# Where the background work stands between the expert rows of a hybrid decoder step: searches just in time, the mixer's second half in the middle periods

## The reference

```
h   = rmsnorm(x);  proj = h @ w_in                       # 1024 x 9240
o_a = gla(q, k, v, log_a)                                # 4 heads, state 128x256
o_b = mlstm(conv(q), conv(k), v, i, f)                   # 4 heads, state 256x256
x   = x + (sigmoid(ga)*norm(o_a)*silu(ag) + sigmoid(gb)*norm(o_b)*sigmoid(bo)) @ w_out
# PEER, per token and per head (8 heads):
q   = rmsnorm(x) @ wq                                    # two halves of 128
s   = top16(q1 @ keys1.T), top16(q2 @ keys2.T)           # 128 keys each side
e   = top16 of the 16x16 sums -> 16 expert numbers of 16384;  g = softmax(sums)
x   = x + sum_k g_k * gelu(x_n . U[e_k]) * V[e_k]        # 128 experts per token
y   = rmsnorm(x)
```

## Time and profile before

| | us |
|---|---|
| median of 3 runs (4853.70 to 4863.44) | 4861.52 |
| the profiled execution's own time | 4865.52 |
| its span | 4863.6 |
| DVE on U rows, L2478, 1024 of them | 1240.9 busy |
| PE on V rows, L2112 | 1378.4 busy |
| PE on the mixer's projections, L2050 | 538.0 busy |
| PE over the span | 3550.3 (73%) |
| DVE over the span | 2815.5 (58%) |
| POOL over the span | 2294.6 (47%) |

### The profile page before, as it was taken

How to read it: one execution, slowest core, us unless ns; L and a number is a source line. 1 busy time by engine, 2 the same in 40 slices (tenths; PEclk the granted TensorE clock), 3 DMA queues, 4 the chain that set the end, 5 groups by cost and what they waited for, 6 DMA issues and landing times.

```text
span 4863.6 us, 37778 instructions
## 1 busy us (share of the span) xinstructions
PE 3550.3 (73%) x11523; PEld 1480.8 (30%) x11523; DVE 2815.5 (58%) x7587; ACT 618.0 (13%) x1261; POOL 2294.6 (47%) x2122
## 2 busy tenths in 40 slices
PE   5698989894433758979889885576577577676577
PEld 3353545353221333324333332122122122121111
DVE  4455655563877873546555563757646746756600
ACT  2111112120000002323233330000000000000000
POOL 0000000000355444647666662477777767777754
PEclk7798989896666879989999997799889998998899
DMA  4213132223577769989989887699999999999998
GB/s 150 56 40 124 51 112 74 89 74 140 167 261 233 259 212 315 348 299 345 358 297 383 311 302 265 235 377 383 365 349 384 378 348 371 384 382 385 356 318 292
DMA packets 454273, 1285.70 MB, mean 264 GB/s; under 512 B 77136, under 2 KB 160648, under 8 KB 452040
## 3 DMA queue, kind: packets, MB, share of 16 engines
q0 software_dynamic: 308768, 1129.45, 63.7%
q1 hardware_dynamic: 145320, 154.07, 9.7%
HBM read 1244.15 MB, written 39.20 MB: 264 GB/s over the span
## 4 chain that ended last, share of the span: by engine, by line
PE 20%; DMA 16%; POOL 14%; DVE 14%; issue 8%; SPq 4%; ACT 1%; DVEq 0%; POOLq 0%; ACTq 0%
DMA c_vb<-in_peer_v,c_idxT 10%; POOL c_vb L1932 7%; PE c_acc L2112 7%; PE c_pj L2050 7%; POOL c_ub L1932 7%; DVE c_ub L2478 4%; DMA c_ub<-in_peer_u,c_idx 3%; SPq L1851 3%; PE c_pj L1974 2%; PE c_pW L1999 2%; DMA out_p_n<-c_extra 1%; DVE c_extra L2333 1%; DVE c_extra L2329 1%; PE c_acc L2036 1%; DVE c_es L2335 1%
## 5 line engine op out<-in xcount | busy, mean ns | idle before, releaser
L2478 DVE CUSTOM_DVE_ANT_0 c_ub<-c_ub,c_h 128x1024 f32<-128x1024 f32 x1024 | 1240.9, 1224 | 925.7 <-DMA c_ub<-in_peer_u,c_idx 919.6
L2112 PE MATMUL c_acc<-c_vb,c_Z 128*32 128x512 f32 x4096 | 1378.4, 663 | 482.2 <-DMA c_vb<-in_peer_v,c_idxT 480.5
L1932 POOL DMA_INDIRECT c_vb<-in_peer_v,c_idxT x1024 | 1121.8, 1095 | 727.3 <-PE c_acc L2112 495.5
L1932 POOL DMA_INDIRECT c_ub<-in_peer_u,c_idx x1024 | 1115.5, 1089 | 726.1 <-DVE c_a L2478 382.7
L2112 PEld LDWEIGHTS c_acc<-c_vb,c_Z 128*32 128x32 f32 x4096 | 250.7, 115 | 1426.5 <-DMA c_vb<-in_peer_v,c_idxT 924.9
L2050 PE MATMUL c_pj<-weights,c_extra 128*128 128x512 f32 (+1 forms) x1280 | 538.0, 570 | 61.8 <-DMA weights<-in_w_in 33.2
L826 PE MATMUL b_pj<-weights,b_hcB 128*128 128x512 f32 (+1 forms) x1280 | 528.9, 571 | 1.1 <-ACT b_s_v L1054 1.1
L482 POOL DMA_DIRECT2D weights<-in_w_in x40 | 36.0, 911 | 672.5 <-PE b_pj L826 658.3
L2050 PEld LDWEIGHTS c_pj<-weights,c_extra 128*128 128x128 f32 x1280 | 242.2, 195 | 359.0 <-issue 352.9
L826 PEld LDWEIGHTS b_pj<-weights,b_hcB 128*128 128x128 f32 x1280 | 249.0, 197 | 256.8 <-issue 249.7
L2015 PE MATMUL c_pZ<-c_subT,c_extra 128*128 128x128 f32 (+1 forms) x288 | 61.8, 349 | 244.7 <-DVE c_extra L2297 244.7
(11 more groups left out here) (435 smaller groups left out, 3501.6 us busy)
## 6 DMA issues: line engine op xcount, KB each, us to landing
weights<-in_w_in POOLq DMA_DIRECT2D x32, 1024.0 KB, 8.1
weights<-in_w_in SPq DMA_DIRECT2D x32, 1024.0 KB, 23.6
c_ub<-in_peer_u,c_idx POOLq DMA_INDIRECT x1024, 6.2
c_vb<-in_peer_v,c_idxT POOLq DMA_INDIRECT x1024, 6.2
b_hcB<-hT_d SPq DMA_DIRECT2D x16, 512.0 KB, 4.9
b_s_C<-in_state_mlstm_c SPq DMA_DIRECT2D x8, 1024.0 KB, 12.6
out_s_c<-b_s_C SPq DMA_DIRECT2D x8, 1024.0 KB
c_extra<-hT_d SPq DMA_DIRECT2D x16, 512.0 KB, 7.2
```

The lines of the kernel that those rows point to most:

```text
L1932: nc.gpsimd.indirect_dma_start(out=out, out_offset=None, in_=io[table], in_offset=bass.IndirectOffsetOnAxis(ap=at, axis=0)).then_inc(loade ...
L2112: last = nc.tensor.matmul(acc[half][j * SUB:(j + 1) * SUB, :], Z[:, lo:lo + SUB], vb[:, turn % RV, half * 512:(half + 1) * 512], start=Fal ...
L2478: nc.vector.tensor_tensor_reduce(ub[:, turn % RU, :], ub[:, turn % RU, :], h2[:, b, :], 1.0, 0.0, ALU.mult, ALU.add, a[:, b, k:k + 1]).the ...
```

## The change

Four things are changed, all in the functions that make the list.

- `begin_items`: "tile_in" (x and the mixer's output) now stands ahead of "search_in" (keys, weights), for tiles 0 and 4. For tile 4 a "pause" follows. A pause is an item that no engine knows; its cost of 30 units leaves slots without background.
- `search_items`: within a head's turn, "best" and "sums" come first, then "sc", "qT" and "q" of the following heads, then "pick". Before, "q" came first and "sc" late.
- `spans`: tiles 1 to 3 are one span, slots 64 to 236. The mixer alone has slots 236 to 448, 1291 units with a pause of 30 behind the issue of its first weights. Tile 4 has slots 448 to 556, tile 5 the slots 558 to 630.
- "h2_in", the load of a tile's normed rows for its U rows, goes from slot 10 to slot 60 in two periods. An assertion says that each U row stands behind its head's "pick".

```diff
 COST = {"out": 3.6, "norm2": 4.5, "hT": 2.4, "q": 3.6, "qT": 0.8, "sc": 0.8, "best": 2.4, "sums": 2.2, "pick": 2.6,
...
-        "num": 1.3, "squares2": 1.0, "cst": 1.3, "mix": 4.5, "s4": 0.8, "mT": 0.5}
+        "num": 1.3, "squares2": 1.0, "cst": 1.3, "mix": 4.5, "s4": 0.8, "mT": 0.5, "pause": 30.0}
 def begin_items(n):
-    order = [("search_in", n, 0)] if n in (0, C0) else []
-    return order + [("tile_in", n, 0)] + [("out", n, k) for k in range(4)] + [("norm2", n, 0), ("x2_out", n, 0)]
+    order = [("tile_in", n, 0)] + [("search_in", n, 0)] if n in (0, C0) else [("tile_in", n, 0)]
+    if n == C0:
+        order += [("pause", n, 0)]
+    return order + [("out", n, k) for k in range(4)] + [("norm2", n, 0), ("x2_out", n, 0)]
 def search_items(n, after_head, ending):
     order = [("hT", n, 0)]
     for t in range(PH + 3):
+        if t >= 3:
+            order += [("best", n, t - 3), ("sums", n, t - 3)]
+        if 2 <= t < PH + 2:
+            order += [("sc", n, t - 2)]
+        if 1 <= t < PH + 1:
+            order += [("qT", n, t - 1)]
         if t < PH:
             order += [("q", n, t)]
...
-        if t >= 3:
-            order += [("best", n, t - 3)]
-        if 1 <= t < PH + 1:
-            order += [("qT", n, t - 1)]
-        if t >= 3:
-            order += [("sums", n, t - 3)]
-        if 2 <= t < PH + 2:
-            order += [("sc", n, t - 2)]
         if t >= 3:
             order += [("pick", n, t - 3)] + after_head(t - 3)
 def mixer_items():
...
     order += [("w_in", 0, g) for g in range(NG)] + [("gates_in", x, 0) for x in range(2)] + [("state_in", 0, 0)]
+    order += [("pause", 0, 0)]
 def rows_items():
...
-            extra[10] = [("h2_in", i + 2, 0)]
+            extra[60] = [("h2_in", i + 2, 0)]
 def merged_schedule():
...
-    spans = [(with_rows_in(chain(range(1, SOON + 1)), 1), 0, SLOTS - 8),
-             (chain(range(SOON + 1, C0)) + mixer_items() + with_rows_in(prepare_items(C0), C0), SLOTS, C0 * SLOTS - 8)]
+    spans = [(with_rows_in(chain(range(1, C0)), 1), SLOTS - 64, 2 * SLOTS - 20),
+             (mixer_items(), 2 * SLOTS - 20, C0 * SLOTS - 64),
+             (with_rows_in(prepare_items(C0), C0), C0 * SLOTS - 64, C0 * SLOTS + 44)]
     for n in range(C0 + 1, TILES):
         items = prepare_items(n)
-        lo = (n - 1) * SLOTS
-        spans.append((with_rows_in(items, n) if n < CHUNKS else items, lo, lo + SLOTS - 10))
+        lo = (n - 1) * SLOTS + (46 if n == C0 + 1 else 0)
+        spans.append((with_rows_in(items, n) if n < CHUNKS else items, lo, (n - 1) * SLOTS + SLOTS - 10))
...
+    for n in range(CHUNKS):
+        for k in range(SLOTS):
+            assert order.index(("u", n, k)) > order.index(("pick", n, k // TOPK))
```

More of the change, by code:

```diff
@@ L1483, in rows_items @@
     return slots
-SOON = 1
 EARLY = 3 * (PH - 1)
```

## The result

The changed kernel takes 4807.42 us (median of 4 runs, 4806.41 to 4816.54), the kernel before 4862.48 beside it (4 runs, 4853.70 to 4887.23): ratio 0.9883, 95% interval 0.9845 to 0.9921. It is faster by 55 us, where 4880 and "a little slower" were forecast. The profiled execution took 4808.24 us, its span is 4806.3.

A forecast was written before the change was run, and what follows sets the result against it. Plain periods were taken as DMA-bound, the mixer as PE and DMA ending nearly together, the dense search as filling no engine. Start and first tile +6, the other stages +11 (1972 against 1961), together +17, gave 4880 us; range 4800 to 4935.

The forecast's parts named there:

- a little slower: Whole kernel: 4880 us, 18 over the 4861.5 before; its own range 4855-4905, chance 0.36.
- The mixer: The 16 mixer steps with 207 slots beside them, 84 fewer: 985 us instead of 1079, bounds 940 and 1010.
- the V waits: In the mixer, PE's 13.2 us of waiting for V rows would go; the sum subtracts 14.
- After the mixer: 192 slots with tiles 4 and 5, w_out and wq: 606 us, bounds 585 and 625; before, 165 slots took 582.
- Stage I: Search of tiles 2 and 3 plus first mixer weights: 381 us for 112.5 slots, before 300 for 56; bounds 362, 405.
- Start and tile 0: Start: -9 us for the mixer's output, -5 for head order; tile 0's U rows +20; together +6.
- The heart of it: A slot taken out of the mixer returns 0.955 us, elsewhere costs 2.75 of DMA; only filling the stalls can pay.
- the cover of the pause: Behind the mixer, 21 pause slots (about 60 us) would just cover state store and w_out, 8.58 to 19.22 plus 39.
- Rival 2: Stages outside the mixer: searches at DMA's pace, weights wholly covered, 362 and 585 us; total 4840, chance 0.14.
- Rival 1: Lean mixer: less DMA beside it, U rows on time, DVE not late, full PE clock; 940 us, total 4835, chance 0.17.
- Rival 3: In-order coupling: PE waits for DVE at scores, deciding past DVE share 0.75; 405, 625, mixer 1010; total 4950, chance 0.23.
- The marks: Periods near 455, 600, 525, 380 us, mixer steps 59-62; forecast falls if DMA outside stays 0.74 or mixer loses under 80.

The follow-up runs named there:

- e4: The kernel before with only the new order of steps within a head: 0.9985, 4853.32 us.
- e7: The changed kernel with the spans of the kernel before, all else kept: 0.9885, 4803.76 us.
- e9: The kernel before with only tile_in ahead of search_in, at tiles 0 and 4: 0.9929, 4823.78 us.
- e1: The changed kernel with the old order of steps within a head for all tiles but tile 4: 0.9902, 4811.47 us.
- e2: The changed kernel without the pause behind tile 4's loads: 0.9899, 4808.9 us.
- e5: The changed kernel with 32 more slots in the mixer's span (from slot 204): 0.9855, 4790.65 us.
- e6: The changed kernel with 32 fewer slots in the mixer's span (from slot 268): 0.9929, 4820.22 us.
- e11: The changed kernel with search_in again ahead of tile_in: 0.9930, 4823.65 us.
- f3: The changed kernel without tile_in first and without both pauses, leaving new spans, head order and h2_in's place: 0.9913, 4825.1 us.
- f2: The kernel before with tile_in ahead of search_in at tile 4 alone: 0.9957, 4837.59 us.
- e10: The kernel before with the two pauses alone: 0.9987, 4852.49 us.
- e8: The changed kernel with the first two groups of mixer weights issued early and the small convolution loads later: 0.9879, 4798.5 us.
- f1: The kernel before with tile_in ahead of search_in at tile 0 alone: 0.9976, 4850.05 us.

## Why the prediction was wrong

The time lies just inside the stated range, 4800 to 4935, but on the other side of "a little slower". The sum said +17 us and the profiles say -57; the 74 between them are these terms.

- **The mixer, 28 us: the term that was mis-sized.** The prediction put 985 us, by "84 x 0.955 = 80 us" and 14 for the V waits. The count of rows (207), the vanished V waits and the other waits that stay (39.0 of 40.8) were right. A row's price was not: it came from one pair at full clock, and the mean of the stage is 307.76 / 290 = 1.06 us. 83 rows at that are 88, and each of the 207 that stay is cheaper by 0.08 (203.09 / 207 = 0.98), 17 more: 105 instead of 80. Projections gave another 7.6 (537.7 to 530.1), and PE's idle time gave 11 instead of 14. Of the 0.08 some is this execution's luck, for in the other mixers a row takes 1.04 to 1.08 us where 280 to 290 stand (e4, e7, e9) and 1.00 to 1.02 where 175 to 239 stand (e1, e2, e5, e6, e11, f3). Some is the clock: matmuls of V rows that took over 900 ns (the mean at granted clock 0.50 is 1061, at 1.00 598) are 78 of 1160 before and 32 of 828 after. Why the rest is cheaper no run shows.
- **After the mixer, 21 us: a term counted in part twice.** 606 was put together from 192 slots at the plain period's 2.93, w_out and wq, and a price for searching. The 2.93 already has one tile's search and idle DMA in it: over 192 slots it is 35 us more than the bare 2.75, and with the 10 for searching 45, where two searches' own loads are 24 by the prediction's 12 a tile. The 21 are the difference. By the DMA account it is the 507 us of DMA work before (583 x 0.87) and 27 slots more at 2.75, 581 us; measured are 585, the lower bound, at a share of 0.99.
- **Stage I, 9 us.** 381 put, 372 measured, DMA at 0.96 (0.93 put). The mechanism held: DMA's idle time was filled, so that the 56 slots more cost only 72 us there, and e6's 32, with nothing left to fill, another 90.
- **Start and tile 0, 13 us.** 9 us were put for the mixer's output at tile 0, and 9.2 came (13.60 to 4.42). 6 of the 13 lie ahead of the change; the tail at tile 0 cost +16 instead of +20.
- **The rest, 3 us**, put at nothing.

**The heart of it**, 0.955 us back for a slot taken out of the mixer and 2.75 paid elsewhere: the second held where DMA was full (2.64 from e5 to e6), the first did not (1.16 to 2.25). The 0.58 a slot that comes back at tile 0 had no place in this price. The net price between e5 and e6 is 0.34 to 0.56 us per slot instead of 1.8. How far it reaches is open: by it 84 slots would cost 29 to 47 us and not 150, and the filled holes outweigh that, but e7, with 74 slots more in the mixer, is as fast as after, and e5, with 32 more, is 14 us faster by the ratios (with intervals that overlap). That new spans as such are no gain was right in a narrow sense: on top of tile_in first they bring nothing (e7), without it some 28 us (f3).

**What the prediction left out** is a value for tile_in at tile 4. It followed the moved rows on SP and priced only the cover of the pause. Alone the move gives 21 us (f2), and the pause nothing (e2, e10). The cover's 39 us for w_out was too long (about 23), because it took the pace of packets of 1 KB for packets of 4 KB; the sum did not hang on it.

**The rivals.** Rival 2, the stages outside fill up, had 362 and 585 us (measured 372 and 585), and is the one that came. Rival 1 had 940 us for the mixer (957), but not by its reason: DVE is as late as before, and the clock is 0.94 (0.93). The two together gave 4795, and rival 2 alone 4840; 4807 lies between. Rival 3, the coupling, did not come: DVE's share in stage I is 0.76 (283.74 of 372), beyond the 0.75 at which it was to decide, and DMA still reached 0.96. The marks that the prediction named: the periods by the first U rows are 439, 586, 517 and 372 us for 455, 600, 525 and 380; DMA outside the mixer did leave 0.74, and the mixer did lose over 80 us, so by these the forecast did not fall, and the sign hung on sizes. A step of the mixer takes 957 / 16 = 60 us and PE does not wait for w_out, as said; for the first mixer weights it waits 31.5 us, not 15 to 20.

## What to carry to other kernels

Where the bytes are fixed and long stretches run at a full DMA, sum up for each stage the idle DMA time, and price a move by what it fills and what it opens. A wait of another engine in a stage with full DMA cost nothing here (27.4 us of PE in e2; 31.5 us less in e8 brought nothing that shows). Take the price of an instruction from its mean in the stage that the sum is about, not from one undisturbed pair. Edits that fill the same hole don't add up: f1, f2 and f3 alone give 12, 21 and 42 us, and the whole change 55.

## What was not expected of the hardware

- Small loads can cost SP as much as large ones; here they are as many packets. The mixer's ten groups of weights (9.4 MB) were issued in 24.72 us, as in the earlier trace rows at the first head (24.55), and ahead of them the 18 small loads of the convolution took 29.5 us, about half of it while PE stood waiting for the weights behind them. From 1861 to 1893.6 SP's queue moved 9672 packets with 0.04 MB in all, from 1893.6 to 1918, for the weights, 9175 packets with 8.08 MB. SP in order of time, in the changed kernel:

```profile
1860.97 13.49 SPq L1833 DMA_DIRECT2D c_extra<-in_conv_w  x8
1874.51 4.71 SPq L1835 DMA_DIRECT2D c_extra<-in_conv_b  x1
1879.26 10.81 SPq L1833 DMA_DIRECT2D c_extra<-in_conv_w  x8
1890.11 0.51 SPq L1835 DMA_DIRECT2D c_extra<-in_conv_b  x1
...
1893.63 24.72 SPq L1855 DMA_DIRECT2D weights<-in_w_in  x10
```

- A full DMA is not one rate: 373 GB/s over the stage behind the mixer (share 0.99), 416 to 418 in the 27 us in which wq landed beside gathers (shares 1.01 and 1.02, e9 and e2), but 170 GB/s in the 14 us in which x and the mixer's output were loaded beside the state store (share 0.99, e9). Why their packets take so long no run shows.
- Two queues that share the DMA engines get equal numbers of packets, not of bytes: 5677 against 5614 with 5.53 against 20.44 MB, for packets of 1 KB against nearly 4.
